# Feed-forward of a decoder trunk: the token norm left out of the up projection, and gate and up of groups 2 to 9 both in seven block products

## The reference, cut to what matters

```python
f = swiglu_ffn(rms_norm(h, norm_g[i, 2]), ffn_w_gate[i], ffn_w_up[i], ffn_w_down[i])
h = h + rms_norm(f, norm_g[i, 3])
# swiglu_ffn: (silu(a @ w_gate) * (a @ w_up)) @ w_down, D_FF = 2816
# rms_norm: x * rsqrt(mean(x * x) + 1e-6) * g
```

## Time and profile before

| what | value |
|---|---|
| three timed runs | 2757.94 to 2757.95 us, median 2757.95 |
| span of the profiled execution, first to last instruction | 2753.8 us |
| median less span | 4.15 us |
| TensorE matmuls busy | 2740.9 us, 15352 matmuls |
| VectorE, ScalarE, GpSimd busy | 1577.9, 1109.0, 776.8 us |
| granted TensorE clock | 1.000 of full speed |
| HBM traffic | 91 GB/s over the span |

### The profile page before, as it was taken

One profiled execution on the slowest core, in us unless ns is written; L12 is line 12 of the kernel. 1 busy time (PEld: TensorE's weight loads), 2 busy tenths in 40 slices (PEclk: granted clock), 3 DMA queues, 4 the chain that ended last, 5 costly groups with the idle time before them and its releaser, 6 DMA issues. The chain is left out here.

```text
span 2753.8 us, 39762 instructions
## 1 busy us (share of the span) xinstructions
PE 2740.9 (100%) x15352; PEld 2350.3 (85%) x15352; DVE 1577.9 (57%) x2157; ACT 1109.0 (40%) x1797; POOL 776.8 (28%) x550
## 2 busy tenths in 40 slices
PE   9999999999999999999999999999999999999999
PEld 7888889888888889988888888889888888889887
DVE  4464676635668676653655455666635465576733
ACT  5322533425257553342443343533424333443422
POOL 0021444303113454330321221543302022254221
PEclk9999999999999999999999999999999999999999
DMA  5323233333620123333332223233333333233331
GB/s 171 92 85 92 79 105 99 97 104 108 167 64 2 40 85 100 103 101 98 106 87 78 82 84 98 86 101 91 102 98 110 90 87 90 77 107 99 90 105 65
DMA packets 448381, 256.37 MB, mean 93 GB/s; under 512 B 9728, under 2 KB 431984, under 8 KB 448112
## 3 DMA queue, kind: packets, MB, share of 16 engines
q1 hardware_dynamic: 446944, 251.69, 31.5%
q10 hardware_dynamic: 1296, 2.75, 0.3%
HBM read 248.11 MB, written 2.10 MB: 91 GB/s over the span
## 5 line engine op out<-in xcount | busy, mean ns | idle before, releaser
L1953 DVE SCALAR_TENSOR_TENSOR w_lo<-w_raw,w_hi 128x1024 fp32r<-128x1024 f32 x461 | 665.1, 1450 | 683.9 <-ACT w_hi L1445 682.7
L1445 ACT ACTIVATE w_hi<-w_raw 128x1024 fp32r<-128x1024 f32 (+1 forms) x460 | 471.2, 1028 | 640.0 <-PE acc L648 544.0
L646 PE MATMUL acc<-a_hi,w_hi 128*128 128x512 f32 (+1 forms) x1688 | 661.9, 392 | 0.3 <-DVE g_lo L2390 0.3
L648 PE MATMUL acc<-a_hi,w_lo 128*128 128x512 f32 (+1 forms) x1688 | 654.8, 388 | 0.0
L647 PE MATMUL acc<-a_lo,w_hi 128*128 128x512 f32 x1496 | 582.7, 389 | 0.0
L648 PEld LDWEIGHTS acc<-a_hi,w_lo 128*128 128x128 f32 x1688 | 317.0, 188 | 65.7
L646 PEld LDWEIGHTS acc<-a_hi,w_hi 128*128 128x128 f32 x1688 | 317.2, 188 | 64.0 <-DVE g_lo L2390 1.2
L647 PEld LDWEIGHTS acc<-a_lo,w_hi 128*128 128x128 f32 x1496 | 281.2, 188 | 56.3 <-issue 1.0
L648 PE MATMUL acc<-hid_hi,w_lo 128*128 128x512 f32 (+1 forms) x704 | 264.5, 376 | 0.0
L647 PE MATMUL acc<-hid_lo,w_hi 128*128 128x512 f32 (+1 forms) x704 | 264.5, 376 | 0.0
L646 PE MATMUL acc<-hid_hi,w_hi 128*128 128x512 f32 (+1 forms) x704 | 264.5, 376 | 0.0
(11 more groups left out here) (439 smaller groups left out, 5451.5 us busy)
## 6 DMA issues: line engine op xcount, KB each, us to landing
w_raw<-ffn_w_gate SPq DMA_DIRECT2D x88, 512.0 KB, 4.0
w_raw<-ffn_w_up SPq DMA_DIRECT2D x88, 512.0 KB, 3.9
w_raw<-gm_w_in SPq DMA_DIRECT2D x64, 512.0 KB, 4.0
w_raw<-ffn_w_down SPq DMA_DIRECT2D x64, 512.0 KB, 3.6
w_raw<-ret_w_in SPq DMA_DIRECT2D x48, 512.0 KB, 3.8
w_raw<-gm_w_out SPq DMA_DIRECT2D x32, 512.0 KB, 3.6
w_raw<-ffn_w_down SPq DMA_DIRECT2D x32, 384.0 KB, 3.2
w_raw<-nsa_w_in SPq DMA_DIRECT2D x21, 512.0 KB, 4.1
```

The source lines that it names most:

```text
L646: pe.matmul(o_bank, lhs_hi, rhs_hi, start=start, stop=False)
L648: return pe.matmul(o_bank, lhs_lo, rhs_hi, start=False, stop=stop)
L1445: act.activation(w_hi[:, slot, rows_of, :], w_raw[:, slot, rows_of, :], ACT.Copy).then_inc(hi_done, 1)
L1953: dve.scalar_tensor_tensor(w_lo[:, slot, rows_of, :], w_raw[:, slot, rows_of, :], 1.0, w_hi[:, slot, rows_of, :].bitcast(f32), ALU.mult, A ...
```

## The change

Group 2 is computed in seven block products too, and in groups 2 to 9 the up pair as well as the gate pair. A pair is now a "half" (`hn`), of which a group has two. The loop runs over pairs of groups, the first and the last written out. In a half TensorE does the three products of plain weight blocks first and the four with weight sums behind them. The up pair's products go to the four `acc` banks, those of group 10's gate units to `st`.

The up projection is no longer multiplied by R. In plain groups VectorE multiplies the up tile in PSUM by the gate tile into `hid_full`; in groups of seven products it joins up into `work` and multiplies the two pairs there. GpSimd makes no such product any more, but eight weight sums per group. The 1e-6 of the second norm is prepared per token: ScalarE squares R with a factor into SS, VectorE inverts SS (128 x 512), and the squares of f are added to it in place of the memset.

`a_full` is made earlier: half of its tiles in the boundary ahead of w_hi of unit 4 and of the root, half behind R. Token sums follow at once on GpSimd; they are rounded in group 1. SP loads units 2 and 3 of the next group after the sums of the up pair.

```diff
-SEVEN_FROM, SEVEN_TO = 3, 10
-SEVENS = SEVEN_TO - SEVEN_FROM
+SEVEN_FROM, SEVEN_TO = 2, 10
+UP_SEVEN = (True, True)
+PAIRS = (SEVEN_TO - SEVEN_FROM) // 2
+PAIR_HALVES = 2 + sum(UP_SEVEN)
+HALVES = PAIRS * PAIR_HALVES
...
+        def groups_of(p):
+            hn = p * PAIR_HALVES
+            for x, up in enumerate(UP_SEVEN):
+                yield p * 2 + (SEVEN_FROM + x), up, hn + (x if x == 0 else 1 + UP_SEVEN[0])
...
+                def after_group(i, up, hg):
+                    for j in range(2):
+                        up_unit(i + 1, j, sums_base(L, hg + 1))
+                    for j in range(2, 4):
+                        up_unit(i + 1, j, sums_base(L, hg + 2) if up else None)
+                def up_pair(p):
+                    for i, up, hg in groups_of(p):
+                        after_group(i, up, hg)
+                for i in range(SEVEN_FROM + 1):
                     for j in range(4):
...
+                        up_unit(i, j)
+                loop(sp, PAIRS, up_pair, 1, 1)
...
+                def seven_half(i, j, hn, x0, x1, y0, y1):
+                    slot0, slot1 = (n0 + j) % SLOTS, (n0 + j + 1) % SLOTS
+                    pe.wait_ge(lo_done, i * 4 + (n0 + j + 1))
+                    block_product(x1[:, first], w_hi[:, slot0, top, :], w_lo[:, slot0, top, :], a_hi[:, top, first], a_lo[:, top, first]).then_inc(s_used, 1)
+                    block_product(x0[:, first], w_hi[:, slot0, bottom, :], w_lo[:, slot0, bottom, :], a_hi[:, bottom, first], a_lo[:, bottom, first]).then_inc(unit_done, 1)
+                    if isinstance(hn, int) and hn == 0:
+                        pe.wait_ge(s_lo, tokens_base(L) + 4)
+                    pe.wait_ge(lo_done, i * 4 + (n0 + j + 2))
+                    block_product(y0[:, first], w_hi[:, slot1, bottom, :], w_lo[:, slot1, bottom, :], t_hi[:, 3, :, :], t_lo[:, 3, :, :]).then_inc(unit_done, 1)
+                    for r, (k, out_half, t) in enumerate([(0, y1[:, first], 0), (2, y1[:, second], 2), (1, x0[:, second], 1), (3, y0[:, second], None)]):
+                        pe.wait_ge(s_lo, sums_base(L, hn) + (r + 1))
+                        rhs_hi = a_hi[:, bottom, second] if t is None else t_hi[:, t, :, :]
+                        rhs_lo = a_lo[:, bottom, second] if t is None else t_lo[:, t, :, :]
+                        block_product(out_half, s_hi_of[k], s_lo_of[k], rhs_hi, rhs_lo).then_inc(s_used, 1)
+                def seven_group(i, up, hg):
+                    if isinstance(hg, int) and hg == 0:
                         pe.wait_ge(r_ready, L["b_mid"] + 1)
                     else:
                         pe.wait_ge(acc_free, i * 4 + (o0 - 2))
...
+                    seven_half(i, 0, hg, st[:, 0, :], st[:, 1, :], tr[:, 0, :], tr[:, 1, :])
+                    if up:
+                        pe.wait_ge(acc_free, i * 4 + o0)
+                        seven_half(i, 2, hg + 1, acc[:, 0, :], acc[:, 1, :], acc[:, 2, :], acc[:, 3, :])
+                    else:
+                        for j in range(2, 4):
+                            plain_unit(i, j)
+                def seven_pair(p):
+                    for i, up, hg in groups_of(p):
...
                 act.wait_ge(stat_h, square_groups(b) + (2 if b else 4))
                 act.activation(work[:, 2, summed], st[:, 0, summed], ACT.Copy).then_inc(h_part, 1)
+                if b % 2:
+                    tokens(b, 0)
                 split_unit(n0 + AHEAD + 1)
                 act.wait_ge(stat_rd, 3 * b + 1)
                 act.activation(r4[:, 0:CH], r4[:, 0:CH], ACT.Sqrt, scale=1.0 / D_MODEL, bias=r4[:, 6:7]).then_inc(root_done, 1)
                 if not into_gmlp(b):
                     rows_of_root(b)
+                if b % 2:
+                    act.wait_ge(r_ready, b + 1)
+                    act.activation(SS[:, :], R[:, :], ACT.Square, scale=(P / (RMS_EPS * D_MODEL)) ** 0.5)
+                    tokens(b, 1)
+            def tokens(b, side):
+                for t in range(side * DT // 2, (side + 1) * DT // 2):
+                    last = act.activation(a_full[:, t, :], h[:, t, :], ACT.Copy, scale=gain[:, gain_of(b), t:t + 1])
+                last.then_inc(tokens_in, 1)
...
+                def p1_copy(hn, x, bank):
+                    act.wait_ge(s_used, used_base(L, hn) + 1)
+                    act.activation(sq[:, x, 0:HALF], bank[:, 0:HALF], ACT.Copy).then_inc(p1_out, 1)
+                def seven_group(i, up, hg, last):
+                    ahead(n0, i, 4, 0, unit_rows(up))
+                    wait(act, acc_free, i * 4 + o0)
+                    p1_copy(hg, 0, st[:, 1, :])
                     ahead(n0, i, 4, 1)
...
+                    ahead(n0, i, 4, 2, unit_rows(not last))
+                    if up:
+                        sums_high(hg + 1)
+                        p1_copy(hg + 1, 1, acc[:, 1, :])
+                    elif not last:
+                        sums_high(hg + 1)
+                    act.wait_ge(m_step, step_base(L, hg) + 4)
                     act.activation(work[:, 0:2, :], work[:, 0:2, :], ACT.Silu).then_inc(silu_done, 2)
                     ahead(n0, i, 4, 3)
+                    if up and not last:
+                        sums_high(hg + 2)
                     if last:
...
+                        act.wait_ge(s_used, used_base(L, HALVES))
...
+                def eps_of_tokens():
+                    dve.wait_ge(tokens_in, 2 * L["layer"] + 2)
+                    dve.reciprocal(SS[:, :], SS[:, :]).then_inc(ss_sum, 1)
+                def gated(i, p):
+                    dve.wait_ge(unit_done, i * 4 + (n0 + 3 + p))
+                    dve.wait_ge(silu_done, i * 2 + (q0 + p + 1))
+                    tile_at = 2 * i + p if isinstance(i, int) else bass.ds(i * 2 + p, 1)
+                    dve.tensor_tensor(hid_full[:, tile_at, :], acc[:, (o0 + 2 + p) % BANKS, :], work[:, p, :], ALU.mult).then_inc(acc_free, 1)
                 def plain(i):
                     for j in range(4):
                         if not begun_split(i, j):
+                            ahead(n0, i, 4, j, unit_rows(i == SEVEN_FROM - 1 and j == 2))
...
+                        if j < 2:
+                            if i:
+                                dve.wait_ge(acc_free, i * 4 + (o0 + j - 1))
+                            bank = st[:, j, :] if i == SEVEN_TO else acc[:, (o0 + j) % BANKS, :]
+                            dve.wait_ge(unit_done, i * 4 + (n0 + j + 1))
+                            dve.tensor_tensor(work[:, j, :], bank, R[:, :], ALU.mult).then_inc(acc_free, 1)
+                        else:
+                            gated(i, j - 2)
+                        if i == SEVEN_FROM - 1 and j == 1:
+                            tokens_low()
+                    if i == 0:
+                        eps_of_tokens()
+                    if i == SEVEN_FROM - 1:
+                        sums_low(0)
+                def join(hn, dst, x, x0, y0, y1, outer, then):
+                    step = step_base(L, hn)
+                    both = work[:, dst:dst + 2, :]
+                    dve.wait_ge(p1_out, p1_base(L, hn) + 1)
+                    dve.wait_ge(s_used, used_base(L, hn) + 4)
+                    dve.tensor_tensor(both[:, :, 0:HALF], by_side(x0), sq[:, x, 0:HALF].unsqueeze(1).broadcast_to([P, 2, HALF]), ALU.add).then_inc(m_step, 1)
                     dve.wait_ge(m_step, step + 1)
+                    dve.tensor_tensor(both[:, :, HALF:SEQ], by_side(y1),
+                                      work[:, dst + 1, 0:HALF].unsqueeze(1).broadcast_to([P, 2, HALF]), ALU.add).then_inc(m_step, 1)
                     dve.wait_ge(m_step, step + 2)
+                    dve.wait_ge(s_used, used_base(L, hn) + 5)
+                    dve.tensor_tensor(work[:, dst + 1, 0:HALF], y0[:, 0:HALF], work[:, dst + 1, HALF:SEQ], ALU.add).then_inc(m_step, 1)
                     dve.wait_ge(m_step, step + 3)
+                    dve.tensor_tensor(both[:, :, HALF:SEQ], by_side(outer), both[:, :, HALF:SEQ], ALU.add).then_inc(then, 2 if then is acc_free else 1)
...
+                def join_gate(i, hg):
+                    dve.wait_ge(acc_free, i * 4 + o0)
+                    join(hg, 0, 0, st[:, 0, :], tr[:, 0, :], tr[:, 1, :], flat(tr[:, :, :]), acc_free)
+                def scale_gate(i):
+                    both = work[:, 0:2, :]
                     dve.wait_ge(acc_free, i * 4 + (o0 + 2))
                     dve.tensor_tensor(both, both, R[:, :].unsqueeze(1).broadcast_to([P, 2, SEQ]), ALU.mult).then_inc(m_step, 1)
+                def join_up(hu):
+                    join(hu, 2, 1, acc[:, 0, :], acc[:, 2, :], acc[:, 3, :], flat(acc[:, 2:4, :]), m_step)
+                def gated_pair(i, hu):
+                    dve.wait_ge(m_step, step_base(L, hu) + 4)
+                    dve.wait_ge(silu_done, i * 2 + (q0 + 2))
+                    tiles = slice(2 * i, 2 * i + 2) if isinstance(i, int) else bass.ds(i * 2, 2)
```

(77 more changed lines are left out.)

174 lines of the change are left out of this document (64 added, 110 removed).

## The result

| | before | after |
|---|---|---|
| median of the timed runs | 2757.94 us | 2792.24 us |
| lowest and highest | 2756.92, 2757.95 | 2788.08, 2796.03 |
| span of the profiled execution | 2753.8 us | 2794.2 us |
| ratio, 95% interval | | 1.0124 [1.0109, 1.0138] |

The change makes the kernel slower by 34 us. The forecast was 2789, in a range of 2742 to 2828, with 0.71 on slower.

What follows compares the result with a forecast made beforehand. The prediction took TensorE's stream, busy 2740.9 of 2753.8 us, as the bound. 2753.8 - 29.7 (gain) + 33.7 (loop stalls) + 26.8 (start) = 2784.6, plus 4.15 around the span gave 2789 us, range 2742 to 2828.

Steps and rivals of the forecast that it cites:

- TensorE's gain: Groups 2 to 9: 36 more pairs in seven products, 0.83 us each, -29.7 us without stalls; a group then lasts 20.16.
- Loop stalls: Up half's first s_lo: VectorE and GpSimd alternate, TensorE waits up to 1.5 us per group, 8.4 per layer, +33.7 in all.
- Start: Beginning of the seven products, one group earlier than before: 6.7 us of stalls per layer, +26.8 over four layers.
- 2.1, 1.7, 0.4, 2.4: Start stalls in us: transposes of the total, w_lo of unit 5, w_lo of unit 9, group 2's first s_lo.
- 4.15: Time in us by which the timed runs exceed the profiled span, taken as untouched by the change.
- 2784.6: Predicted span in us: 2753.8 - 29.7 + 33.7 + 26.8.
- Rival 1: Loop: lock waits fit, no steady stall; 2740 with a small start lag, chance 0.17; 2755 with the full lag, 0.10.
- Rival 2: Loop: GpSimd's sum wins ties against the scaling, 2811, or at the paired product too, some 2850; chance 0.22.
- Rival 3: Loop: VectorE products of two SBUF inputs take no lock, stall about 0.8 us per group, 2773; chance 0.08.
- VectorE's 2.1 us behind the Silu: Loop group: VectorE idles 1.06 + 1.05 us, since w_lo waits for w_hi, queued on ScalarE behind the Silu.

Runs made afterwards that it cites:

- e1: The changed kernel with GpSimd adding only a quarter of each weight sum and filling the rest with a constant (computation left out); 2751.03 us, ratio 0.9977.
- e3: The changed kernel with GpSimd's first token sum also waiting for VectorE's last square sum of the boundary; 2780.71 us, ratio 1.0084.
- e5: The changed kernel with the second half of a_full made behind w_hi of unit 6 instead of in the boundary; 2777.06 us, ratio 1.0071.
- e6: The changed kernel with VectorE's reciprocal of SS at the end of group 10 instead of group 0; 2778.25 us, ratio 1.0074.
- e4: The changed kernel with the up pairs plain again in groups 2 to 9, everything else kept; 2787.86 us, ratio 1.011.
- e2: The changed kernel with ScalarE making w_hi of the next unit 2 ahead of the gate's Silu instead of behind it; 2791.9 us, ratio 1.0125.
- e8: The changed kernel with the start edits of e3, e5 and e6, and up pairs in seven products only in groups 2, 4, 6 and 8; 2745.94 us, ratio 0.996.
- e7: The changed kernel with the three start edits of e3, e5 and e6 together; 2768.69 us, ratio 1.0037.

## Why the prediction was right

**TensorE's gain, -29.7.** Held: e1's groups last 20.16.

**Loop stalls, +33.7 predicted, 31.4 measured.** The mechanism, its place (the first s_lo of the up half) and its size came as laid out. In layer 0 the waits are 0.55, 1.21, 1.23, 1.22, 1.24, 1.14, 1.65 = 8.2 against 8.4 predicted as 0, 0, 0.9 and five of 1.5 (the first of the eight without one); the settled group 21.48 against 21.66; the s_lo start at 3.0 against 3.3. The other layers have 8.2, 7.2 and 7.8. What was off is the approach: the first waits come early, since the chain is already late from group 2, and the settled wait is 1.2: TensorE wants the s_lo 14.4 after the gate's start (451.68 + 0.12 - 437.40), as laid out, but has it at 15.6 (453.02 - 437.40) and not at 15.8.

**Start, +26.8 predicted, 25.9 measured**: in layer 0 2.1, 1.7, 0.4, 2.4 predicted and 2.11, 1.63, 0.51, 2.04 measured. e3, e5 and e6 each remove what they were named for. The reciprocal took 3.34; the price was taken from the same operation elsewhere, and held.

**What stood in no term.** Half-clock stretches, 8.7 us, and the restart behind each wait, about 42 x 0.10 = 4 us. With them -29.7 + 31.4 + 25.9 + 8.7 + 4 = 40.3, and the profiled spans differ by 40.4. The count is not as exact as that looks: ahead of the transposes 0.33 pass even without a wait (e3), and not 0.23, so each of those waits is 0.1 too long in it.

**What made up for it.** The forecast added 4.15 for what lies around the span. That term was wrong in kind. In after it is 2796.03 - 2794.2 = 1.8, and in all 13 runs of before beside e1 to e4 it is 1.8 to 2.1, while the span itself goes from 2753.7 to 2757.2. The profiled execution of before was one of the shortest, and 2.2 of the 4.15 is that. So the forecast is nearer than its terms. The sum for the span, 2784.6, was 9.6 short of the profiled execution: 13 of stretches and restarts not foreseen, less 3 that loop and start were put too high. The wrong term made up 2.3 of that (4.15 - 1.84), and 3.8 fell away because the profiled execution was the longest of after's four. The forecast ended 3 short, and that much of its nearness is luck.

**The rivals.** Rival 1, with the lock waits fitting, needs s_lo before 2.5 in a settled group; it came at 3.0. Nor would that start have been enough: in e2 it came at 1.8, the four s_lo then took 3.60, and the waits stayed (29.2 against 31.4). Rival 2's order, with the sum ahead of the scaling, is not in the trace: the scaling went first at 433.20, and the sum issued at 433.32 took 2.25. Rival 3 fell to the sum of 443.40.

**Where my model of the loop was wrong although its number held.** I named VectorE's 2.1 us behind the Silu as lost, and on that basis expected e2 to bring 20 to 30 us. It brought none. From e1 and e2 together I take that a group is bound less by a chain with a gap in it than by how many instructions that exclude each other must be placed before the s_lo, so that closing a gap moves a collision; that is argued from these two runs, not shown by one of its own.

## What to carry to other kernels

Before moving work from a full engine to two half-idle ones, add to the busy time of each what it waits for the other: here 15.9 us of VectorE work in a 20.16 us group left no room, because eight GpSimd instructions took a turn each; half as many in every second group cost nothing. That made a gain of 0.4% out of a loss of 1.2%, once the pieces that the change had put early were placed behind the instruction for which TensorE waits (e8). And look at what a wait of 2 us does behind itself: in e3 the waits removed were 8.5 us and the gain 11.5.

## What the runs showed of the hardware

- The granted clock went to its lower level behind waits of TensorE of about 2 us, between stretches in which it had been full, and 1.4 to 1.5 us were lost each time. It did so behind some of these waits and not behind others: 6 of 8 in the profiled execution of after, 3 of 4 in e1, 5 of 9 in e2, 1 of 4 in e3, 5 of 8 in e4, 3 of 4 in e5, 1 of 4 in e6; e7 and e8 have no such waits. No stretch lies behind unit 5's waits of up to 1.8 us or the loop's usual ones of up to 1.7. What decides is open; no run was made for it.
- One more stretch, at 776 to 789 us, stands in layer 1's mixer in e1 and e3 to e8, and not in before, after and e2. It begins at the end of 32 matmuls of 31 columns or within 0.5 us of it: in e5 there is no wait ahead of them, in the others one of 1.0 us. Behind that wait it costs 1.6 us.
- The spread of after's runs may come from such stretches: the granted clock of its four runs lies between 0.996 and 0.997, that of before at 0.998 to 1.000. That is not shown: only one run of each kernel has a trace, and the rounded clocks don't put after's four runs in order.
- Behind a wait, the second matmul starts 0.10 us later than the usual distance (431.54 to 431.76 for 256 columns).
- A sum of 128 columns on GpSimd still waits a whole VectorE instruction: e1's issued at 449.02 takes 1.29 beside the w_lo of 448.76, and 0.46 alone.
